# Forming the low parts of 210 weight tiles on VectorE instead of GpSimd in a two-block transformer kernel

## What is computed

```
for l in range(2):                       # first block
    h = rms_norm(x) * (1 + scale) + shift          # scale, shift, gate: silu(c) @ w_mod + b_mod
    p = h @ w_in                                   # Fourier, pooling, q, k, v, gate columns
    y = concat(fourier_mix, pool_mix, differential attention over latent and context keys)
    x = x + gate * ((y * silu(g)) @ w_out)
for l in range(2):                       # second block
    h = rms_norm(x) * (1 + sc1) + sh1              # modulation: silu(c) @ ada_w + ada_b
    x = x + g1 * (hybrid_mixer(h @ w_in) @ w_out)  # retention heads and HGRN2 heads
    h = rms_norm(x) * (1 + sc2) + sh2
    x = x + g2 * ((silu(causal_conv(h @ w_gate)) * (h @ w_val)) @ w_down)
return rms_norm(x)
```

## Time and profile before

| what | value |
|---|---|
| median of 3 runs | 2266.0 us (2264.14 to 2266.96) |
| the profiled execution | 2262.56 us, span 2261.3 us |
| TensorE busy | 2136.1 us |
| VectorE busy | 1318.4 us |
| ScalarE busy | 799.1 us |
| GpSimd busy | 856.2 us |
| mean granted TensorE clock | 0.975 of full speed |

### The profile page before, as it was taken

The page is one execution under the profiler, slowest core; times in us unless marked ns, Lnnn a source line. Parts: engine busy times, 40 slices in busy tenths (PEclk is TensorE's granted clock), DMA queues, the critical chain, the costliest instruction groups (busy, mean ns, idle before and its releaser), DMA issues.

```text
span 2261.3 us, 26237 instructions
## 1 busy us (share of the span) xinstructions
PE 2136.1 (94%) x10540; PEld 1739.4 (77%) x10540; DVE 1318.4 (58%) x1574; ACT 799.1 (35%) x1133; POOL 856.2 (38%) x458
## 2 busy tenths in 40 slices
PE   6999988997999888999999999999999999999998
PEld 1778777884777776888887888887888887888886
DVE  5576767465566656485376741876585376631336
ACT  2445655313555542423333322322423333222221
POOL 0331223333322444432244544554433244544442
PEclk9999999997999998999999999999999999999999
DMA  7321212123222235533233543543443232433332
GB/s 276 121 84 56 66 57 66 57 84 121 84 75 73 77 91 148 162 119 111 67 102 104 157 124 112 165 120 95 149 140 103 85 93 85 151 112 95 101 98 78
DMA packets 313736, 240.89 MB, mean 107 GB/s; under 512 B 6928, under 2 KB 289936, under 8 KB 312976
## 3 DMA queue, kind: packets, MB, share of 16 engines
q1 hardware_dynamic: 294464, 169.48, 25.8%
q0 software_dynamic: 18432, 67.12, 8.7%
q10 hardware_dynamic: 720, 2.62, 0.4%
HBM read 237.10 MB, written 2.10 MB: 106 GB/s over the span
## 4 chain that ended last, share of the span: by engine, by line
PE 75%; issue 8%; DVE 7%; ACT 5%; POOL 3%; DMA 1%; SPq 0%; DVEq 0%; ACTq 0%; POOLq 0%
PE ps L551 59%; POOL w_lo_second L534 2%; PE ps L2020 2%; ACT a_p L1351 1%; PE ps L1085 1%; PE ps L1738 1%; PE ps L1117 1%; PE ps L971 1%; PE ps L1090 1%; DVE mod_products_in L654 1%; DMA first_mod<-in_w_mod_first 1%; PE ps L1128 1%; DVE attention_stats L1529 1%; POOL w_lo_first L534 1%; DMA w_raw_first<-in_w_in 1%
## 5 line engine op out<-in xcount | busy, mean ns | idle before, releaser
L534 POOL TENSOR_TENSOR w_lo_second<-w_raw_second,w_hi_second 128x1024 fp32r<-128x1024 f32 x168 | 419.4, 2501 | 530.5 <-ACT w_hi_second L526 529.7
L551 PE MATMUL ps<-h_second_hi,w_hi_second 128*128 128x512 f32 x1216 | 491.0, 404 | 18.1 <-DVE h_second_lo L798 13.5
L551 PE MATMUL ps<-h_second_hi,w_lo_second 128*128 128x512 f32 x1216 | 477.7, 393 | 0.0
L551 PE MATMUL ps<-h_second_lo,w_hi_second 128*128 128x512 f32 x1216 | 477.6, 393 | 0.0
L551 PEld LDWEIGHTS ps<-h_second_hi,w_hi_second 128*128 128x128 f32 x1216 | 230.8, 190 | 76.3 <-issue 15.1
L534 POOL TENSOR_TENSOR w_lo_first<-w_raw_first,w_hi_first 128x1024 fp32r<-128x1024 f32 x64 | 161.8, 2529 | 328.8 <-ACT w_hi_first L526 328.3
L551 PEld LDWEIGHTS ps<-h_second_hi,w_lo_second 128*128 128x128 f32 x1216 | 230.7, 190 | 49.5
L551 PEld LDWEIGHTS ps<-h_second_lo,w_hi_second 128*128 128x128 f32 x1216 | 231.3, 190 | 47.3 <-issue 1.9
L551 PE MATMUL ps<-h_hi,w_hi_first 128*128 128x512 f32 (+1 forms) x640 | 247.7, 387 | 13.7 <-DVE h_lo L798 4.7
L551 PE MATMUL ps<-h_hi,w_lo_first 128*128 128x512 f32 (+1 forms) x640 | 228.4, 357 | 0.0
L551 PE MATMUL ps<-h_lo,w_hi_first 128*128 128x512 f32 (+1 forms) x640 | 228.1, 356 | 0.0
(11 more groups left out here) (278 smaller groups left out, 3657.6 us busy)
## 6 DMA issues: line engine op xcount, KB each, us to landing
w_raw_second<-in_w_in SPq DMA_DIRECT2D x64, 512.0 KB, 5.7
w_raw_first<-in_w_in SPq DMA_DIRECT2D x48, 512.0 KB, 3.9
mod_w_mixer<-in_ada_w_turned POOLq DMA_DIRECT2D x46, 512.0 KB, 5.1
w_raw_second<-in_w_gate SPq DMA_DIRECT2D x44, 512.0 KB, 4.6
w_raw_second<-in_w_val SPq DMA_DIRECT2D x44, 512.0 KB, 4.1
w_raw_down<-in_w_down SPq DMA_DIRECT2D x32, 704.0 KB, 4.8
mod_w_ffn<-in_ada_w_turned POOLq DMA_DIRECT2D x32, 512.0 KB, 5.0
mod_w_in<-in_w_mod_turned POOLq DMA_DIRECT2D x28, 512.0 KB, 3.9
```

The lines of the kernel that those rows point to most:

```text
L534: k.nc.gpsimd.tensor_tensor(lo, raw, hi.bitcast(F32), ALU.subtract).then_inc(k.sem.weight_split, 1)
L551: last = tensor.matmul(k.ps[:, bank, 0:count], w[:, cut], x[q][:, first:first + count], start=(q == 0 and n == 0), stop=(q == t.k - 1 and ...
```

## The change

VectorE forms the low part of 210 of the 264 tiles: "in" from its 4th tile on (21 of 24 in each layer), "in2" from its 5th on (28 of 32), "ffn" from its 5th on in the first half (18 of 22) and all 22 in the second half, and all 8 of each "down". GpSimd keeps the first tiles after each norm, and the tiles of "out" and "out2" (54 in all). A second semaphore counts VectorE's splits, and a table `self.split` tells for each tile which semaphore and count to wait for.

```diff
+        self.split, splits, at = [], [0, 0], {}
+        for t in self.tiles:
+            i = at[t.stage] = at.get(t.stage, -1) + 1
+            name = t.stage[0]
+            first = {"in": 3, "in2": 4, "ffn": 0 if t.stage[-1] else 4, "down": 0}.get(name, KT)
+            by = int(i >= first)
+            splits[by] += 1
+            self.split.append(((s.weight_split, s.weight_split_v)[by], splits[by]))
...
-                self.load_after.append((s.weight_used if before == self.last_tile(("in", 1)) else s.weight_split, before + 1))
+                self.load_after.append((s.weight_used, before + 1) if before == self.last_tile(("in", 1)) else
+                                       self.split[before])
...
 def split_tile(k, u):
+    if k.split[u][0] is not k.sem.weight_split:
+        return
...
+def split_tile_vector(k, u):
+    if k.split[u][0] is not k.sem.weight_split_v:
+        return
+    raw, hi, lo = k.buffers[u]
+    k.nc.vector.wait_ge(k.sem.weight_rounded, u + 1)
+    if k.split_after[u]:
+        k.nc.vector.wait_ge(*k.split_after[u])
+    k.nc.vector.tensor_tensor(lo, raw, hi.bitcast(F32), ALU.subtract).then_inc(k.sem.weight_split_v, 1)
...
-        tensor.wait_ge(k.sem.weight_split, u + 1)
+        tensor.wait_ge(*k.split[u])
...
+        if stage[0] in ("ffn", "down") and u + 1 < len(k.tiles):     # linear_vector, ahead of evacuate(u)
+            split_tile_vector(k, u + 1)
...
+        if s % 4 == 1 and i + 1 < len(own):                          # first_vector, at the head of step s
+            split_tile_vector(k, own[i + 1])
...
-            prepare_gpsimd(k, l, h, own[s // 4] + 2, KT * l + max(0, (s - 66) // 4))
+            prepare_gpsimd(k, l, h, k.split[own[2]][1], KT * l + max(0, (s - 66) // 4))
...
+        if i + 1 < len(own):                                         # mixer_vector, at the head of turn i
+            split_tile_vector(k, own[i + 1])
```

More of the change, by code:

```diff
@@ L160 @@
     condition_landed condition_ready
-    weight_landed0 weight_landed1 weight_landed2 second_landed0 second_landed1 second_landed2 weight_rounded weight_split x_used weight_used evacuated_a evacuated_v
+    weight_landed0 weight_landed1 weight_landed2 second_landed0 second_landed1 second_landed2 weight_rounded weight_split weight_split_v x_used weight_used evacuated_a evacuated_v
     mod_landed0 mod_landed1 mod_done
```

## The result

The changed kernel takes 2233.2 us (median of 4 runs, 2230.2 to 2236.3) against 2266.5 us of the kernel before: a ratio of 0.9856, 95% interval 0.9841 to 0.9871, or 33 us faster. The forecast was 2248, 18 us faster, with 2236 as the lower end. The kernel was run twice more beside other kernels: 0.9872 (0.9857 to 0.9886) and 0.9899 (0.9884 to 0.9915), 29 and 22 us faster.

A forecast was written before the change was run, and what follows sets the result against it. TensorE, busy 94% of the span, was taken to bound the kernel. Idle time 14.7 plus clock 6 less new waits 3 gave 17.7, say 18 us, off the 2266.0 us median: 2248 us, range 2236 to 2262.

The forecast's parts named there:

- The mechanism: Mostly in the two "in" stages: GpSimd splits hold VectorE for whole instructions, so TensorE waits and then runs at half clock.
- term 6: New waits for VectorE's added splits, in "in" and around the heads' preparations: 3 us lost, between 0 and 16.
- term 5: Half-clock stretches behind the idle stretches of both "in" stages return to full clock: 6 us gained, between 0 and 9.8.
- Terms 1 to 4: TensorE idle time removed: first "in" 4.1 (first head) and 2.0 (modulation sum), second "in" 5.2, "in2" 3.4; together 14.7 us.
- Late splits in the feed-forward: Rival: splits behind modulation sums come 1.3 us late at 29 gate tiles, 37 us, giving 2285 us; chance 0.10.
- The waits only change hands: Rival: TensorE finds ScalarE not ready instead, no clock gain, only 4.4 us saved, 2262 us; chance 0.15.
- More than summed: Rival: all of the clock, no new waits, about 5 us of short VectorE waits: 29.5 us saved, 2236 us; chance 0.15.

The follow-up runs named there:

- in_only: Against the kernel before, only the 42 tiles of the two "in" stages moved to VectorE; 25 us faster than the kernel before.
- rest_only: Against the kernel before, only the 168 tiles of "in2", "ffn" and "down" moved to VectorE, "in" left on GpSimd; 2260.6 us.
- idle_steps: Changed kernel with splits of four tiles in each first-layer feed-forward half repeated 2 to 5 times more; 2282.3 us.
- ffn_reads: Changed kernel plus a GpSimd reading subtraction beside the 82 VectorE splits in "ffn" stages; 2344.9 us, 102 over the changed kernel.
- gpsimd_reads: Changed kernel plus an unused GpSimd subtraction reading SBUF at the 42 places of "in" from which splits moved; 2263.7 us.
- ffn_twice: Changed kernel with each of the 82 VectorE splits in "ffn" stages made twice; 2260.2 us, 21 over the changed kernel.

## Why the prediction was wrong

*The mechanism* held. GpSimd's splits held VectorE at the places named, the holds are gone, and putting the holds of "in" alone back undoes the gain that "in" brought. Wrong were sizes: the gain came out 15 us over the forecast, by term 6, by short waits that no term had, and by term 5 with 5 us of chance on top.

*Terms 1 to 4* forecast 4.1 + 2.0 + 5.2 + 3.4 = 14.7 us of idle time. Matmul by matmul the same places gave 4.07, 1.97, 5.3 (1.64 + 1.59 + 2.07) and 3.4 (2.26 + 1.15): 14.7.

*Term 6, new waits,* is the first step that failed. I put 3 us on it; in the trace one wait in "in" grew with the moved splits, by 0.2 us. *The short waits* are the second: eight waits in "in", for VectorE and for what stands behind it, shrank by 0.2 to 0.7 us each, 4.5 us together. They are as short in in_only, and in rest_only all eight are as long as before. Waits at the norms, which also differ between the profiles of the changed kernel, took about 1.6 us of that back, so that idle time fell by 3.0 us more than the 14.7. I had left those waits out, gave them 5 us in a rival, and gave the forecast none. What led to term 6 was "the splits beside the heads' preparation leave as many places where VectorE was held before": VectorE was held for 238 us, and had that much to give. The sign to look at was in the profile before: 2773 ns on average for a sum that takes 1275 unheld. I took the free durations for the added work but took only some 135 us off for the holds, and expected VectorE to be busy for 1450 us; 238 went, and it was 1349.

*Term 5, the clock,* was probably mis-sized. I took 6 of 9.8 us. Over the 12 runs of the changed kernel span x (1 - clock) averages 52.4 us, over the 38 of the kernel before 61.9: 9.5 us, near my upper bound, but the scatter of the runs alone gives it a 95% interval of some 6 to 13 us. My reason to take less, "smaller waits stand around them", is not settled either. Behind the idle stretches left, of 1.4 and 1.5 us, the clock stays full in the first two profiles, as behind the 1.86 us of idle_steps; in the third it is at half from 1.9 us behind the wait of 1.51 us that ends at 289.9:

```profile
291.80:295.20 3.40, 3.40 (x11) 2.84 (x12) 1.92 (x2) 0.52 (x1) 0.00 (x0) 0.51 0.33 133
```

Whether that wait or chance brought it, no run tells.

So what lasts is 18.4 us in span x clock (2203.0 less 2184.6, averaged over the same runs) and 9.5 of clock, 28 us, against a forecast of 18. The first measurement had 5 us on top: its four runs lost 46 us to the clock, those of the other two groups 54 and 57. That part is scatter between groups of runs, not the change, and it is what put the time below 2236, by chance. Without it, at 2266.5 - 28 = 2238.5, the range would have held and the forecast still been 10 us too high. What makes the clock fall in one execution of the same kernel and not in another, and why one group of runs loses less than the next, stays open.

*Late splits in the feed-forward* did not come. The slack I worked out, 0.5 us, measured 0.67. Its price if it does come was too low: 37 us forecast, 102 measured in ffn_reads, because there the split behind the sum is held as well, which makes 2.95 us of idle time out of 1.3, and because I left out the clock.

*The waits only change hands:* no. TensorE's four waits for ScalarE at the scores fell from 3.7 us to 3.0, with everything else.

*More than summed,* at 2236 us, with chance 0.15, was the case that came: it has all of the clock, no new waits and the short waits. What went beyond it in the first group is the scatter. (The Trainium skill's page "SBUF — State Buffer", section "SBUF: two separate sides", gives the hold in the direction in which it mattered here and names two-input operations. The runs agree, and show it for a one-input `CAST` of `act_value` too: 1445 ns on average before, 428 after, which fits the page's other case, a VectorE operation in its fast mode; that `CAST` runs in this mode no run shows.)

## What to carry to other kernels

Before pricing work that moves from GpSimd to VectorE, compare each VectorE group's mean with its shortest member. In the trace of before the difference, summed over all groups, is 339 us; that is an upper bound, since some members differ for other reasons and some are held by what stays on GpSimd. 238 us came back, against 269 us of work that was added. Where an engine is held in an order written by hand, small waits behind it can go together with the large ones, here 4.5 us beside 14.7, so the large ones alone are too small a sum. Price a stall with the clock behind it (here 1.86 and 2.4 us of idle time cost none, 2.95 did at 16 of 18 places, 3.12 and more each time), remember that half clock also comes where TensorE did not idle, and judge a difference of under 10 us by idle time in the profiles rather than by a median of four runs.

## What the runs showed of the hardware

- A GpSimd subtraction that reads SBUF holds a VectorE operation that reads two inputs from SBUF, and the `CAST` below, until it has ended, whoever needs the result. In the trace of before 26 of the 32 modulation sums of "ffn" start beside one and end about 1.08 us behind its end, nearly their free length of 1.28 us; two `a_q` went from 1.94 to 5.74 us in gpsimd_reads, a split from 1.22 to 3.22 in ffn_reads. Even an operation on 128 x 2 elements in SBUF, 160 ns alone, took up to 1778; seven of 40 were held.
- A GpSimd fill (0.90 us, reads nothing) held no VectorE operation: 1.02 us for the combination with 0.82 us of a fill to go, and 1348.8 us of VectorE's busy time against 1349.4 without the fills.
- VectorE operations that read PSUM were not held. In the trace of before, 32 of the 44 products `act_value`, which read PSUM, start while a GpSimd subtraction runs, and take 687 ns (median) like the 12 others. Of the 44 `CAST` of `act_value` 40 start so and take 1596 ns, the 4 others 427.
- The mean clock of one unchanged kernel ranged from 0.969 to 0.976 over 19 runs, and its time from 2274.3 to 2261.6 us with it.
- The first matmul behind a wait takes longer at full clock too: 0.50 us in ffn_twice against 0.39, and the matmuls behind a 0.60 us wait came 0.9 us later.
